# Layer B of a hybrid decoder step: decay rows by a transfer from DRAM, keys and values turned by VectorE's 32 x 32 transposes and on-chip transfers instead of by TensorE

## The chip, the cores and the metric

The kernel runs on one core of a Trainium2 chip. The metric is the device time of one execution in microseconds. Engines: TensorE (PE in the profile, its weight loads PEld), VectorE (DVE), ScalarE (ACT), GpSimd (POOL) and SyncE (SP), which here only issues DMAs.

## What is computed

One step of a two-layer decoder trunk for a prompt of 1024 tokens and a sample group of 8 x 4 tokens, all in float32. Layer A is windowed attention and is not touched. Layer B is gated DeltaNet: a short convolution on q, k and v, a decay per head, and the delta rule in chunks. The prompt part of it, per head and chunk of the kernel (128 tokens; the reference has 64, with the same result in exact arithmetic):

```
gc = cumsum(g)                                   # decay exponents of the chunk
decay[i, j] = exp(gc[i] - gc[j]) where j <= i
lmat = strict((k * beta) k^T * decay)
u, w = solve(I + lmat, [v * beta, k * beta * exp(gc)])
aqk  = (q k^T) * decay
v_new = u - w S
o     = (q * exp(gc)) S + aqk v_new
S     = S * exp(gc_last) + (k * exp(gc_last - gc))^T v_new
```

There are 8 heads of 128 columns and 8 chunks a head. Around it stand one projection (W_in), 4-head attention into 256 memory tokens, a gate and an output projection.

## The kernel before

The program is written in phases with a stream of instructions per engine and semaphores by hand. Layer B's phase (before.py from line 1888) works on "groups": group G is head G // 2, chunks 0 to 3 or 4 to 7, so there are NG_ = 16 of them. The main loop runs over G = 0 to 16 and in it over 16 slots. In pass G every engine does, slot by slot, the matrix part of group G (the products k k^T and q k^T, and the blockwise inverse of I + lmat, up to 128 x 128), the preparation of the next groups (convolution, norms, decays), and the state recurrence of group G - 1 (RSLOT: per chunk a step "a" with k S and q S, a step "b" with the inverse, a step "c" with the output and the state update). Between these TensorE issues "units": one product of 128 x 128 weights with 352 columns (in the profile two instructions, L2104) of the input projection of the head after. The table `slots` says how many units stand before and behind the recurrence's step in each slot: 36 in a pass up to G = 12, then 20, 16 and 20, since there is not much of the projection left; pass 16 has the rest and only the recurrence.

What the change touches:

- `to` (L2155) with r = None issues four TensorE transposes into one PSUM bank (L2160). Four results a group are made so. "ra": the cumulated decays `gc` of a chunk, one column broadcast to 128 x 128 and turned, so each partition has the row of all 128 exponents (slot 5, for G + 1). "kt" (slot 7) and "vt" (slot 15): keys and values of the four chunks, tokens to partitions. "ot" (slot 10): normed outputs; this one stays.
- VectorE reads them (`turned`, L2553): ra with the mask added into `ATs` (L2559), kt times a factor per token into `kdec` (L2567), vt times a factor into `vb` (L2570).
- ScalarE turns ATs to decays (`exps`, L2379, slot 7) behind the logs of norms (`norm_logs`, slot 5). kdec and vb are needed by the recurrence of the group, in the pass after.
- The inverse: VectorE's base steps on 16 x 16 blocks (`base_step`, L2629 and L2631) for group G + 1 in slots 12 to 15 of pass G and for group G in slots 0 to 5, then `base_turned` (L2636), which TensorE waits for in slot 7 (level x4, L2178). zz4, x5, zz5, x6, zt6 follow; `base_rows` (L2616, L2617) is a long transpose in slot 11 for the next group.
- PSUM banks 3 to 7 go round in the order of the list `work`; a step may be issued once the bank's fifth last user was read.
- SP loads weight blocks of 512 KB into a ring of four (`Ring.load`, L137), each once the block four before is used up, and stores a head's final state (`state_away`, L2076).
- GpSimd squares q and k, scales outputs, does the sample part of the convolution, and in passes 0 to 11 issues copies of window caches from DRAM to DRAM (`copy_part`).

Head by head the working data lie in fixed places: `qkvT` holds q, k and v of two heads with columns of the head on partitions and tokens along the row.

Of the kernel before, what the change touches and what calls it, by code (L numbers as in the profile page):

```python
# [27 lines left out]
HB = 8  # L28
# [86 lines left out]
class Chain:  # L115


    def __init__(self, nc, eng, name):
        self.eng, self.sem, self.n = eng, nc.alloc_semaphore(name), 0
# [27 lines left out]
def build(nc, ins, outs):  # L147
# [10 lines left out]
    part = dram("part", [2, SEQ, OW])  # L158
    memT_kept = dram("memT_kept", [P, KD * NMEM])
# [365 lines left out]
    def _(dve):  # L525
        own = Chain(nc, dve, "in_dve")
# [603 lines left out]
    def _(dve):  # L1130
        own = Chain(nc, dve, "dve_a")
# [168 lines left out]
    def _(pool):  # L1300
        own = Chain(nc, pool, "pool_a")
# [445 lines left out]
    def _(dve):  # L1747
        own = Chain(nc, dve, "wa_dve")
# [165 lines left out]
    S = take(2, P)  # L1914
    S_of = lambda h, c: S3[(NT * h + c) % 3]
# [14 lines left out]
    vb = mv[:, 0:2, :].rearrange("p a b -> p (a b)").rearrange("p (c e) -> p c e", e=P)  # L1930
    flat = lambda v: v.rearrange("p a b -> p (a b)")
# [49 lines left out]
    work = [(0, "ss"), (0, "ra"), (0, "kk"), (0, "qk")]  # L1981
# [12 lines left out]
    for n, (g, name) in enumerate(work):  # L1994
# [6 lines left out]
     cvs, spread, base, tap, chosen) = (  # L2001
# [4 lines left out]
            "diagonals_spread", "base_steps", "first_taps", "blocks_chosen"))  # L2006
# [43 lines left out]
    slots += [[(0, 1)] * 16, [(0, 2)] * 4 + [(0, 1)] * 12]  # L2050
# [24 lines left out]
    def _(sp):  # L2075
# [18 lines left out]
    def _(pe):  # L2094
# [102 lines left out]
        def chunk_step(g, s):  # L2197
# [9 lines left out]
            elif x == "b":  # L2207
                readout(pe, g, f"zt{LEVELS - 1}")
                readout(pe, g, f"ks{c}" if c else "vt")
                to(g, f"tr{c}", [(MT[:, c, :], r_sb[:, c % 2, :] if c else vb[:, c, :])])  # L2210
            elif x == "c":
                readout(pe, g, f"tr{c}")
                to(g, f"av{c}", [(ATs[g % 3][:, cl, :], vn[:, c % 2, :])])
                to(g, f"su{c}", [(kdec[:, c, :], vn[:, c % 2, :])])

        def turned(G, name):
# [11 lines left out]
            elif name == "kt":  # L2228
                to(G, "kt", [(ch(k_, c), None) for c in cs])
            elif name == "vt":  # L2230
                to(G, "vt", [(ch(v, c), None) for c in cs])
# [51 lines left out]
        turned(0, "ra")  # L2283
        for u in units[PER_HEAD + KD:PER_HEAD + 2 * KD]:
            unit(*u)
# [21 lines left out]
    def _(act):  # L2307
        def gate_piece(j):
# [3 lines left out]
            else:  # L2312
                act.wait_ge(ring.used, B2 + i + 1)
            if i == 2 and part_ == 0:
# [64 lines left out]
        def exps(G):  # L2379

            readout(act, G, "ra")
# [6 lines left out]
        def outputs(g):  # L2388

            b = left(act, g, "ot")  # L2390
            nc.scalar.activation(brT[:, g // 2, g % 2 * 512:(g % 2 + 1) * 512], b[:, :], ACT.Copy,
                                 scale=onw).then_inc(rd_act, 1)

# [64 lines left out]
        for G in range(NG_ + 1):  # L2458
            for s in SLOTS:
# [14 lines left out]
                if G == NG_ and s == 15:  # L2474
                    out_roots(NG_ - 1)
                for u in ended(units_at(G, s)):
# [12 lines left out]
    def _(dve):  # L2489
        own = Chain(nc, dve, "b_dve")  # L2490
# [62 lines left out]
        def turned(G, name):  # L2553
# [11 lines left out]
            elif name == "kt":  # L2565
                dve.wait_ge(hdv, 3 * G + 3)
                nc.vector.tensor_tensor(kdec[:, cs, :], bk(b), factors_of[:, KD_, cs].unsqueeze(2)  # L2567
                                        .to_broadcast([P, 4, P]), ALU.mult).then_inc(rd_dve, 1)
            elif name == "vt":
                nc.vector.tensor_tensor(vb[:, cs, :], bk(b), factors_of[:, KN, cs].unsqueeze(2)  # L2570
                                        .to_broadcast([P, 4, P]), ALU.mult).then_inc(rd_dve, 1)
# [66 lines left out]
        def chunk_step(g, s):  # L2638
# [4 lines left out]
            if x == "a" and c:  # L2643
                readout(dve, g, "vt")
# [86 lines left out]
        turned(0, "ra")  # L2731
# [1026 lines left out]
```

## Time and profile before

| | us |
|---|---|
| median of 3 runs | 2113.65 |
| lowest, highest | 2112.19, 2114.21 |
| the profiled execution, its own time | 2113.68 |
| its span in the profile | 2111.6 |
| TensorE busy | 2072.5 (98%) |
| VectorE busy | 997.2 (47%) |
| ScalarE busy | 697.7 (33%) |
| GpSimd busy | 454.6 (22%) |

The mean granted TensorE clock over the span is 0.993. Layer B's phase runs from about 1069 us to 1674 us; the first pass of its loop begins at about 1123 us, a pass takes about 34 us, and pass 13 begins at about 1555 us. In the profile "L2160" is a line of kernel.py; PSUM is "bank", all of SBUF is one tile "arena", so rows are told apart by their line.

### The profile page before, as it was taken

To read this page: it belongs to the slowest core of one execution; us is meant where nothing else is said; L and a number is where in the kernel's file an instruction comes from. 1 tells how busy PE (TensorE), PEld (TensorE's weight loads), DVE (VectorE), ACT (ScalarE), POOL (GpSimd) and SP (SyncE) were. 2 spreads that over 40 slices of the span, in tenths; PEclk is the share of its full clock that TensorE was granted. 3 is DMA by queue.
4 is the path that set the end of the run, shared out by engine and by line. 5 is a ranking of instruction groups with operands and counts; after the bars stand their busy time and mean duration, and the time that the engine had idled before them with its cause. 6 is when DMAs were issued, how large, how long until landed. Compare 5 with 4: busy or idle time off the path is not lost. (4 is left out here: it accounts for less than half of the span.)

```text
span 2111.6 us, 36594 instructions
## 1 busy us (share of the span) xinstructions
PE 2072.5 (98%) x14446; PEld 1487.2 (70%) x14446; DVE 997.2 (47%) x2664; ACT 697.7 (33%) x1631; POOL 454.6 (22%) x639
## 2 busy tenths in 40 slices
PE   8999999999999999999999999999999999999998
PEld 6888888888888887555466777767666666665444
DVE  5234354354435345331238777777876133332252
ACT  4121321322131122231135555555564344532101
POOL 0522232222223213300023134322331200020000
PEclk9999999999999999999999999999998999999999
DMA  7411301211131127668412122222210461134451
GB/s 235 161 43 41 107 27 51 80 41 43 41 97 37 50 83 223 237 202 255 131 31 74 73 95 83 93 87 82 73 48 13 137 256 31 41 105 134 134 161 50
DMA packets 210238, 210.34 MB, mean 100 GB/s; under 512 B 14261, under 2 KB 181653, under 8 KB 209150
## 3 DMA queue, kind: packets, MB, share of 16 engines
q1 hardware_dynamic: 198070, 148.27, 23.7%
q0 software_dynamic: 12000, 59.73, 7.4%
q8 instruction: 117, 1.92, 0.4%
q14 instruction: 51, 0.42, 0.1%
HBM read 179.56 MB, written 68.23 MB: 117 GB/s over the span
## 5 line engine op out<-in xcount | busy, mean ns | idle before, releaser
L887 PE MATMUL bank<-arena 128*128 128x256 f32 (+1 forms) x2688 | 631.7, 386 | 0.0
L887 PEld LDWEIGHTS bank<-arena 128*128 128x128 f32 x2688 | 494.5, 190 | 75.3
L2104 PE MATMUL bank<-arena 128*128 128x352 f32 x1296 | 452.5, 470 | 0.1
L2104 PEld LDWEIGHTS bank<-arena 128*128 128x128 f32 x1296 | 220.8, 191 | 71.4 <-issue 1.0
L2909 PE MATMUL bank<-arena 128*128 128x352 f32 x576 | 176.4, 459 | 0.0
L3399 PE MATMUL bank<-arena 128*128 128x512 f32 x360 | 167.5, 599 | 0.0
L2162 PEld LDWEIGHTS bank<-arena 128*128 128x128 f32 x864 | 129.9, 194 | 45.7 <-DVE arena L2646 3.7
L2909 PEld LDWEIGHTS bank<-arena 128*128 128x128 f32 x576 | 106.6, 190 | 53.3
L1341 POOL TENSOR_TENSOR arena<-arena 128x272 f32<-128x272 f32 (+1 forms) x48 | 31.5, 656 | 507.4 <-ACT arena L1061 487.4
L2162 PE MATMUL bank<-arena 128*128 128x128 f32 x864 | 135.0, 280 | 1.5 <-DVE arena L2646 1.0
L1323 POOL TENSOR_TENSOR arena<-arena 128x512 f32<-128x512 f32 x96 | 122.8, 1279 | 11.3 <-POOL arena L1323 0.9
L1660 PE MATMUL bank<-arena 128*128 128x512 f32 x248 | 118.6, 601 | 1.8 <-DMA arena<-in_w_out_a 1.8
L2508 DVE SCALAR_TENSOR_TENSOR arena<-arena 128x512 f32<-128x512 f32 x144 | 114.1, 793 | 0.7
L3399 PEld LDWEIGHTS bank<-arena 128*128 128x128 f32 x360 | 64.4, 189 | 70.4 <-issue 70.4
L924 PE MATMUL bank<-arena 128*128 128x128 f32 x396 | 79.3, 276 | 8.4 <-ACT arena L1096 7.2
L1096 ACT ACTIVATE arena<-arena 128x256 f32<-128x256 f32 (+1 forms) x128 | 59.9, 468 | 82.3 <-DVE arena L1185 74.5
L1169 DVE COPY arena<-bank 128x256 f32<-128x256 f32 (+1 forms) x208 | 78.8, 384 | 14.0 <-PE bank L924 14.0
L2631 DVE TENSOR_TENSOR arena<-arena 128x120 f32<-128x120 f32 (+14 forms) x240 | 76.2, 318 | 8.3
L924 PEld LDWEIGHTS bank<-arena 128*128 128x128 f32 x396 | 53.2, 141 | 29.8 <-ACT arena L1096 8.4
L1058 ACT COPY arena<-bank 128x272 f32<-128x272 f32 (+1 forms) x48 | 18.3, 381 | 166.7 <-PE bank L887 166.7
L1660 PEld LDWEIGHTS bank<-arena 128*128 128x128 f32 x248 | 42.2, 189 | 38.4 <-issue 34.7
L2808 POOL TENSOR_TENSOR arena<-arena 128x512 f32<-128x512 f32 x32 | 36.0, 1136 | 139.9 <-ACT arena L2352 139.9
(432 smaller groups left out, 2754.1 us busy)
## 6 DMA issues: line engine op xcount, KB each, us to landing
arena<-in_w_in_a SPq DMA_DIRECT2D x48, 512.0 KB, 5.2
arena<-in_w_in_b SPq DMA_DIRECT2D x40, 512.0 KB, 7.5
arena<-in_cache_win_k SPq DMA_DIRECT2D x48, 256.0 KB, 6.1
arena<-in_cache_win_v SPq DMA_DIRECT2D x48, 256.0 KB, 4.7
out<-arena SPq DMA_DIRECT2D x40, 256.0 KB, 3.4
arena<-in_w_mem_kv SPq DMA_DIRECT2D x16, 512.0 KB, 8.1
arena<-in_cache_mem_k SPq DMA_DIRECT2D x32, 256.0 KB, 4.3
arena<-in_cache_mem_v SPq DMA_DIRECT2D x32, 256.0 KB, 4.2
```

Of the source, the lines that this page charges most:

```text
L887: m = nc.tensor.matmul(o[:, 0:hi - lo], w, y, start=k == 0 and i in (0, 1, 3, 5), stop=k == KH - 1, skip_group_check=i in (2, 4, 6))
L924: m = nc.tensor.transpose(tB[e % 2][:, c * P:(c + 1) * P], src, ident)
L1096: nc.scalar.activation(pr[:, x % 2, c:256], sS[:, x % 2, c:256], ACT.Exp, bias=nm, accum_out=l).then_inc(p_done, 1)
L1169: nc.vector.tensor_copy(dst, tB[e % 2][:, lo:lo + w]).then_inc(t_read, 1)
L1323: nc.gpsimd.tensor_tensor(*v).then_inc(w_sums, 1)
L1660: i = nc.tensor.matmul(bank[BY0 + half][:, :], brT[:, k, n * P:(n + 1) * P], wo_a(k)[:, half * 512:(half + 1) * 512], start=j == 0, stop=j ...
L2104: m = nc.tensor.matmul(bank[j % 3][:, 0:PART], ring.slots[:, (B1 + b) % RING, k, :], part_in(k, part_), start=k == 0, stop=k == KD - 1)
L2162: m = nc.tensor.matmul(o[:, c * P:(c + 1) * P], l, r, start=True, stop=True)
L2508: x = nc.vector.scalar_tensor_tensor(out=dst, in0=src, scalar=cw, in1=dst, op0=ALU.mult, op1=ALU.add)
L2631: nc.vector.tensor_tensor(m[:, :, :, 0:j], m[:, :, :, 0:j], t, ALU.subtract).then_inc(base, 1)
L2909: m = nc.tensor.matmul(bank[part_][:, 0:PART], ring.slots[:, (B2 + b) % RING, k, :], part_in(k, part_), start=k == 0, stop=k == KD - 1)
L3399: m = nc.tensor.matmul(bank[BY0 + half][:, :], brT[:, k, n * P:(n + 1) * P], wo_b(k)[:, half * 512:(half + 1) * 512], start=j == 0, stop=j ...
```

## The change

Decay rows. Before group 0 TensorE turns `gc` once (64 columns: 8 chunks of 8 heads, "gr"), VectorE copies the 64 x 128 result, SP stores it in DRAM (`gc_kept`). For each group from 1 on SP loads four rows of it, broadcast to all 128 partitions, straight into ATs (`rows_to`: 128 x 4 pieces of 512 bytes, at the head of pass G for G + 1), and VectorE adds the mask to them in place (`mask_rows`) at the head of slot 6. ra remains for group 0 alone.

Keys and values. VectorE's stream transpose turns each 32 x 32 block in place of TensorE's 128 x 128 (`kv_turned`: one instruction of 128 x 512 for k in slot 6, one for v in slot 7, for group G + 1). The blocks must then change places across partitions: SP does it with 16 transfers a group, each of 32 partitions by 1 KB (`turned_to`). ScalarE scales the pieces into kdec and vb, two instructions a chunk, in slots 2 to 5 of the pass after (`scale_turned`). kt and vt are gone, with their slots and banks.

SP's program is written anew: the weight loads, the state stores and the new transfers in one order by pass. In pass 15 the four slots with two units are the last four and no longer the first four.

TensorE in pass 1, slots 5 to 8, before. L2160 is a quad of transposes (ra, then kt), L2162 x2 or x4 a product pair or kk, L2104 a unit, L2178 the inverse's x4:

```order
L2160 MATMUL bank<-arena 128x128 x4
L2104 MATMUL bank<-arena 128x352
L2162 MATMUL bank<-arena 128x128
L2104 MATMUL bank<-arena 128x352 x2
L2162 MATMUL bank<-arena 128x128 x2
L2104 MATMUL bank<-arena 128x352
L2160 MATMUL bank<-arena 128x128 x4
L2178 MATMUL bank<-arena 32x16 x16
L2104 MATMUL bank<-arena 128x352 x2
L2162 MATMUL bank<-arena 128x128 x4
```

And after, from the unit of slot 4 on (L2150 is the unit, L2208 a product, L2224 the inverse):

```order
L2150 MATMUL bank<-arena 128x352 x2
L2208 MATMUL bank<-arena 128x128
L2150 MATMUL bank<-arena 128x352 x2
L2208 MATMUL bank<-arena 128x128 x2
L2150 MATMUL bank<-arena 128x352
L2224 MATMUL bank<-arena 32x16 x16
L2150 MATMUL bank<-arena 128x352 x2
L2208 MATMUL bank<-arena 128x128 x4
```

Both quads are gone; the order of the rest is the same.

VectorE in a later pass, slot 5 to the head of slot 6, before: the read of ra (L2559) stands ahead of the last base steps, then the base's transpose and the two reads of the recurrence:

```order
L2508 SCALAR_TENSOR_TENSOR arena<-arena 128x512
L2559 TENSOR_TENSOR arena<-bank7,arena 128x512
L2629 TENSOR_TENSOR arena<-arena 128x8x2
L2631 TENSOR_TENSOR arena<-arena 128x8x2
L2629 TENSOR_TENSOR arena<-arena 128x8
L2631 TENSOR_TENSOR arena<-arena 128x8
L2636 STREAM_TRANSPOSE arena<-arena 128x128
L2652 TENSOR_TENSOR arena<-bank4,arena 128x128
```

After, the same place; the mask (L2660) comes behind the base's transpose (L2725):

```order
L2582 SCALAR_TENSOR_TENSOR arena<-arena 128x512
L2718 TENSOR_TENSOR arena<-arena 128x8x2
L2720 TENSOR_TENSOR arena<-arena 128x8x2
L2718 TENSOR_TENSOR arena<-arena 128x8
L2720 TENSOR_TENSOR arena<-arena 128x8
L2725 STREAM_TRANSPOSE arena<-arena 128x128
L2660 TENSOR_TENSOR arena<-arena 128x512
L2741 TENSOR_TENSOR arena<-bank3,arena 128x128
```

The base's transpose moved ahead of the 128 x 512 operation, the recurrence's reads did not.

VectorE right behind it, slots 6 and 7, before: the state update, four small factors, the read of kt (L2567) and of x4 (L2587), a convolution step:

```order
L2659 SCALAR_TENSOR_TENSOR arena<-arena,bank5 128x128
L2533 SCALAR_TENSOR_TENSOR arena<-arena 128x4
L2535 TENSOR_TENSOR arena<-arena 128x4
L2536 TENSOR_TENSOR arena<-arena 128x4
L2537 TENSOR_SCALAR arena<-arena 128x4
L2567 TENSOR_TENSOR arena<-bank6,arena 128x512
L2587 TENSOR_TENSOR arena<-bank7,arena 128x4x16
L2508 SCALAR_TENSOR_TENSOR arena<-arena 128x512
```

After:

```order
L2748 SCALAR_TENSOR_TENSOR arena<-arena,bank4 128x128
L2650 STREAM_TRANSPOSE arena<-arena 128x4x4x32
L2607 SCALAR_TENSOR_TENSOR arena<-arena 128x4
L2609 TENSOR_TENSOR arena<-arena 128x4
L2610 TENSOR_TENSOR arena<-arena 128x4
L2611 TENSOR_SCALAR arena<-arena 128x4
L2676 TENSOR_TENSOR arena<-bank5,arena 128x4x16
L2650 STREAM_TRANSPOSE arena<-arena 128x4x4x32
L2582 SCALAR_TENSOR_TENSOR arena<-arena 128x512
```

One transpose stands ahead of the factors, one behind the read of x4, and the read of kt is gone.

The core of the diff:

```diff
-    PREP = {5: ("ra",), 7: ("kt",), 8: ("kk",), 9: ("qk",), 15: ("vt",)}
-    NEXT = ("ra", "kk", "qk")
+    PREP = {8: ("kk",), 9: ("qk",)}
+    NEXT = ("kk", "qk")
+    AT_MASK = 6
+    AT_TURN = {6: 0, 7: 1}
+    SCALE_AT = {2: 0, 3: 1, 4: 2, 5: 3}
-    slots += [[(0, 1)] * 16, [(0, 2)] * 4 + [(0, 1)] * 12]
+    slots += [[(0, 1)] * 16, [(0, 1)] * 12 + [(0, 2)] * 4]
@@ SP
+        def rows_to(g):
+            h, c0 = g // 2, GR[g % 2][0]
+            if g > 2:
+                left(sp, g - 3, f"av{GR[(g - 3) % 2][1] - 1}")
+            sp.wait_ge(rows_away, 16)
+            if g > 1:
+                sp.wait_ge(rows_in, 16 * (g - 1))
+            src = gc_kept.rearrange("(c h) i -> h c i", h=HB)[h, c0:c0 + 4]
+            sp.dma_start(ATs[g % 3], src.unsqueeze(0).to_broadcast([P, 4, P])).then_inc(rows_in, 16)
+        def turned_to(g):
+            sp.wait_ge(turnd, 2 * (g + 1))
+            after(sp, kvs, 4 * g)
+            for b in range(4):
+                for a in range(4):
+                    sp.dma_start(kv_words[quarter(b), 256 * a:256 * a + 256],
+                                 turned_in[g][quarter(a), 256 * b:256 * b + 256]).then_inc(kv_in[g % 2], 16)
-        for b in range(3 * HB):
-            if b % 3 == 2 and b // 3 >= 3:
-                state_away(b // 3 - 3)
-            ring.load(sp, B1 + b + 1)
-        state_away(HB - 3)
-        ring.load(sp, B2 + RING)
+        for b in range(7):
+            weights(b)
+        readout(sp, 0, "gr")
+        sp.dma_start(gc_kept, gc_rows).then_inc(rows_away, 16)
+        turned_to(0)
+        for G in range(NG_):
+            if G + 1 < NG_:
+                rows_to(G + 1)
+            if G % 2 and G < NG_ - 1:
+                weights(3 * (G // 2) + 8)
+                weights(3 * (G // 2) + 9)
+            if G + 1 < NG_:
+                turned_to(G + 1)
+            if G % 2 == 0:
+                weights(3 * (G // 2) + 7)
@@ TensorE, tr0 and the state update
-                readout(pe, g, f"ks{c}" if c else "vt")
+                if c:
+                    readout(pe, g, f"ks{c}")
+                else:
+                    pe.wait_ge(kvs, 4 * g + 1)
+                pe.wait_ge(kvs, 4 * g + cl + 1)
                 to(g, f"su{c}", [(kdec[:, c, :], vn[:, c % 2, :])])
@@ ScalarE
+            if G:
+                act.wait_ge(masked, G)
+            else:
+                readout(act, 0, "ra")
+        def scale_turned(g, cl):
+            w, c = hd[:, g // 2 % 2], GR[g % 2][0] + cl
+            if not cl:
+                act.wait_ge(kv_in[g % 2], 256 * (g // 2 + 1))
+                act.wait_ge(hdv, 3 * g + 3)
+                if g > 1:
+                    left(act, g - 2, f"su{GR[g % 2][1] - 1}")
+            wide = lambda v: v.rearrange("p (a x) -> p a x", x=32)
+            nc.scalar.activation(wide(kdec[:, c, :]), kv_back[:, :, 0, cl, :], ACT.Copy, scale=w[:, KD_, c:c + 1])
+            nc.scalar.activation(wide(vb[:, c, :]), kv_back[:, :, 1, cl, :], ACT.Copy,
+                                 scale=w[:, KN, c:c + 1]).then_inc(kvs, 1)
@@ VectorE
+        def kv_turned(G, i):
+            h, gr = G // 2, G % 2
+            dve.wait_ge(sild, 3 * G + 2 + i)
+            if G and not i:
+                dve.wait_ge(kv_in[(G - 1) % 2], 256 * ((G + 1) // 2))
+            x = qkvT[:, h % 2, 1 + i, gr * 512:(gr + 1) * 512].rearrange("p (c b x) -> p c b x", c=4, b=4)
+            nc.vector.transpose(turned_kv[G][:, :, i].rearrange("p b c x -> p c b x"), x).then_inc(turnd, 1)
+        def mask_rows(G):
+            dve.wait_ge(rows_in, 16 * G)
+            nc.vector.tensor_tensor(ATs[G % 3], ATs[G % 3], wide4(mat(M_GE)), ALU.add).then_inc(masked, 1)
@@ VectorE, ahead of pass 0
         turned(0, "qk")
+        kv_turned(0, 0)
+        kv_turned(0, 1)
```

## Rows read from the trace of the kernel before

**Rows 1.** The page, part 1: busy us (share of the span) and instructions

```profile
PE 2072.5 (98%) x14446; PEld 1487.2 (70%) x14446; DVE 997.2 (47%) x2664; ACT 697.7 (33%) x1631; POOL 454.6 (22%) x639
```

**Rows 2.** Stretches: length, busy by engine (instructions), granted clock, DMA share, GB/s

```profile
1263.40:1297.70 34.30, 34.30 (x399) 24.19 (x398) 25.92 (x76) 19.31 (x46) 15.44 (x34) 1.00 0.29 95
...
1131.30:1543.30 412.00, 411.59 (x4842) 292.00 (x4842) 313.17 (x885) 226.23 (x540) 134.56 (x270) 1.00 0.23 83
1543.30:1640.00 96.70, 90.81 (x1163) 64.31 (x1162) 70.49 (x213) 46.94 (x117) 22.84 (x43) 0.93 0.12 30
```

**Rows 3.** L2160's instructions, then TensorE's timeline: start, length, instruction, [idle before]

```profile
L2160 PE MATMUL bank<-arena x256: 272/273/421, 1106.6 to 1673.5; 128*128 128x128 f32 x128
...
1226.02 0.60 PE L2160 MATMUL bank<-arena 128*128 128x128 f32 x4
1226.45 0.76 PE L2104 MATMUL bank<-arena 128*128 128x352 f32 x2
...
1229.49 0.60 PE L2160 MATMUL bank<-arena 128*128 128x128 f32 x4
1230.02 0.44 PE L2178 MATMUL bank<-arena 32*32 32x16 f32 x32
...
1232.66 0.73 PE L2178 MATMUL bank<-arena 32*32 32x16 f32 x64
...
1236.54 0.38 PE L2162 MATMUL bank<-arena 128*128 128x128 f32 x2
```

**Rows 4.** VectorE's timeline in the same pass, slots 5 to 7

```profile
1227.85 0.68 DVE L2559 TENSOR_TENSOR arena<-bank,arena 128x512 f32<-128x512 f32 x1
1228.45 0.16 DVE L2629 TENSOR_TENSOR arena<-arena 128x16 f32<-128x16 f32 x1
...
1229.29 0.31 DVE L2636 STREAM_TRANSPOSE arena<-arena 128x128 f32<-128x128 f32 x1
...
1230.99 0.21 DVE L2587 TENSOR_TENSOR arena<-bank,arena 128x64 f32<-128x64 f32 x1
```

**Rows 5.** VectorE's groups by shape, 1130 to 1620 us: busy, mean ns, idle before

```profile
L2617 DVE STREAM_TRANSPOSE arena<-arena 128x1920 f32<-128x1920 f32 x15 | 32.6, 2172 | 0.0
...
L2631 DVE TENSOR_TENSOR arena<-arena 128x112 f32<-128x112 f32 x15 | 13.8, 922 | 0.5
...
L2631 DVE TENSOR_TENSOR arena<-arena 128x120 f32<-128x120 f32 x15 | 4.3, 285 | 0.5
```

**Rows 6.** ScalarE's timeline: exps in slot 7, recurrence in slots 2 and 5

```profile
1232.24 1.28 ACT L2384 ACTIVATE arena<-arena 128x128 f32<-128x128 f32 x4
...
1256.08 0.40 ACT L2419 ACTIVATE arena<-arena 128x128 f32<-128x128 f32 x1 [2.77 <-DVE arena L2652]
...
1261.76 0.27 ACT L2414 COPY arena<-bank 128x128 f32<-128x128 f32 x1 [1.48 <-PE bank L2162]
```

**Rows 7.** VectorE's timeline, slot 8

```profile
1233.62 0.69 DVE L2562 TENSOR_TENSOR arena<-arena,bank 128x512 f32<-128x512 f32 x1 [1.76 <-ACT arena L2384]
...
1234.51 0.35 DVE L2646 SCALAR_TENSOR_TENSOR arena<-bank,arena 128x128 f32<-128x128 f32 x1
```

**Rows 8.** Timeline ahead of and in pass 0, VectorE and TensorE

```profile
1130.20 0.31 DVE L2636 STREAM_TRANSPOSE arena<-arena 128x128 f32<-128x128 f32 x1
...
1130.71 0.44 PE L2178 MATMUL bank<-arena 32*32 32x16 f32 x32
```

**Rows 9.** TensorE's timeline, passes 13 and 14

```profile
1581.40 0.64 PE L2170 MATMUL bank<-arena 64*32 64x64 f32 x16 [1.74 <-DVE arena L2604]
...
1584.28 1.22 PE L2162 MATMUL bank<-arena 128*128 128x128 f32 x4
...
1589.53 0.77 PE L2162 MATMUL bank<-arena 128*128 128x128 f32 x2 [0.69 <-DVE arena L2646]
```

**Rows 10.** SP's DMAs: the state's issue in ns, from issue to landing in us

```profile
L2078 SPq DMA_DIRECT2D out<-arena x8: 356/357/357, 1214.4 to 1663.1; - x8
...
DMA to landing us min/median/max: 1.5/8.5/11.6
```

More of the change, by code:

```diff
@@ L1914, in build @@
     S = take(2, P)
+    gc_rows = r_sb[0:64, 1, :]
     S_of = lambda h, c: S3[(NT * h + c) % 3]
@@ L1930, in build @@
     vb = mv[:, 0:2, :].rearrange("p a b -> p (a b)").rearrange("p (c e) -> p c e", e=P)
+    turned_in = [brT[:, HB - 2, 0:1024]] * (2 * HB - 1) + [xpad[:, 0, 0:1024]]
+    turned_kv = [w.rearrange("p (b i c x) -> p b i c x", b=4, i=2, c=4) for w in turned_in]
+    kv_words = sb[:, ZM[0]:ZM[0] + 1024]
+    kv_back = kv_words.rearrange("p (a i c x) -> p a i c x", a=4, i=2, c=4)
     flat = lambda v: v.rearrange("p a b -> p (a b)")
@@ L1980, in build @@
     reader_of = lambda n: "act" if n in ("ss", "ot") or n[:2] in ("qs", "tr") else "dve"
-    work = [(0, "ss"), (0, "ra"), (0, "kk"), (0, "qk")]
+    work = [(0, "ss"), (0, "ra"), (0, "gr"), (0, "kk"), (0, "qk")]
     for G in range(NG_ + 1):
@@ L2000, in build @@
     (pd, pr_, wk, rd_act, rd_dve, cvd, sild, sqd, hdv, hda, exd, mt0, onm, sqo, fac, tails, sqrt_o, cstep, xzero,
-     cvs, spread, base, tap, chosen) = (
+     cvs, spread, base, tap, chosen, rows_away, rows_in, masked, turnd, kv_even, kv_odd, kvs) = (
         sem(f"b_{n}") for n in (
@@ L2005, in build @@
             "out_factors", "conv_tails", "out_roots", "conv_steps", "buffers_zeroed", "samples_convolved",
-            "diagonals_spread", "base_steps", "first_taps", "blocks_chosen"))
+            "diagonals_spread", "base_steps", "first_taps", "blocks_chosen",
+            "rows_kept", "rows_loaded", "rows_masked", "kv_turned", "kv_moved_even", "kv_moved_odd", "kv_scaled"))
+    kv_in = (kv_even, kv_odd)
     s_out = stored["state"]
@@ L2213, in chunk_step, with decay_rows @@
                 to(g, f"av{c}", [(ATs[g % 3][:, cl, :], vn[:, c % 2, :])])
+                pe.wait_ge(kvs, 4 * g + cl + 1)
                 to(g, f"su{c}", [(kdec[:, c, :], vn[:, c % 2, :])])
+        def decay_rows():
+            o = bank_free(0, "gr")
+            nc.tensor.transpose(o[0:64, 0:P], gc[:, 0:64], ident).then_inc(wk, 1)
         def turned(G, name):
@@ L2283, in _ @@
         turned(0, "ra")
+        decay_rows()
         for u in units[PER_HEAD + KD:PER_HEAD + 2 * KD]:
@@ L2313, in gate_piece @@
                 act.wait_ge(ring.used, B2 + i + 1)
+            if i == 1 and part_ == 0:
+                act.wait_ge(kvs, 4 * NG_)
             if i == 2 and part_ == 0:
@@ L2475, in _ @@
                     out_roots(NG_ - 1)
+                if G < NG_ and s in SCALE_AT:
+                    scale_turned(G, SCALE_AT[s])
                 for u in ended(units_at(G, s)):
@@ L2564, in turned, with decay_rows @@
                 nc.vector.tensor_tensor(at_, at_, bk(b), ALU.mult).then_inc(rd_dve, 1)
[L2565 to L2571, printed above, removed]
+        def kv_turned(G, i):
[3 more added lines that the diff above has]
+                dve.wait_ge(kv_in[(G - 1) % 2], 256 * ((G + 1) // 2))
+            if G == NG_ - 1 and not i:
+                dve.wait_ge(cvd, 3 * NG_)
+                dve.wait_ge(tap, 3 * (NG_ - 2))
+            x = qkvT[:, h % 2, 1 + i, gr * 512:(gr + 1) * 512].rearrange("p (c b x) -> p c b x", c=4, b=4)
+            nc.vector.transpose(turned_kv[G][:, :, i].rearrange("p b c x -> p c b x"), x).then_inc(turnd, 1)
+        def decay_rows():
+            b = left(dve, 0, "gr")
+            nc.vector.tensor_copy(gc_rows, b[0:64, 0:P]).then_inc(rd_dve, 1)
+        def mask_rows(G):
+            dve.wait_ge(rows_in, 16 * G)
+            nc.vector.tensor_tensor(ATs[G % 3], ATs[G % 3], wide4(mat(M_GE)), ALU.add).then_inc(masked, 1)
         def matrix_step(G, s):
@@ L2731, in _ @@
         turned(0, "ra")
+        decay_rows()
         for w in range(CW):
@@ L2742, in _ @@
             for s in SLOTS:
+                if s == AT_MASK and G + 1 < NG_:
+                    mask_rows(G + 1)
                 if G < NG_:
@@ L2746, in _ @@
                     chunk_step(G - 1, s)
+                if s in AT_TURN and G + 1 < NG_:
+                    kv_turned(G + 1, AT_TURN[s])
                 if s == AT_INV:
```

33 lines of the change are left out of this document (16 added, 17 removed).

## The prediction

> **What bounds the kernel now.** I read first the busy time by engine [rows 1]: TensorE's matmul record covers 98% of the span, no other engine passes 47%. That alone says little, so I looked at the stage that the change touches in stretches [rows 2]. From 1131.3 to 1543.3 us TensorE is busy 411.6 of 412.0 us at full granted clock; a group of four chunks (one pass of the loop over G) takes 34.3 us, VectorE works 25.9 us of it and ScalarE 19.3. The stretch from 1543.3 to 1640 is different: TensorE is busy 90.8 of 96.7 us and the mean granted clock is 0.93. So I count twelve "dense" groups (G = 1 to 12), where what TensorE does not issue is time gained, and treat G = 0 and the tail (G = 13 to 15) by themselves. I write slot s for the sixteen steps of a group.
>
> **What is removed from TensorE.** 16 times kt, 16 times vt, 15 times ra: 47 quads of transposes. L2160 has 256 records of one pass each [rows 3], that is 64 quads (the rest are ot and ra(0)). Price of one quad: the quad at 1226.02 is followed by the next product at 1226.45, so 0.43 us [rows 3]. The quad at 1229.49 is followed by the inverse's tiled products at 1230.02, 0.53 us [rows 3]; I put the 0.10 more down to the step to tiled products, which stays, and take 0.43 there too. A dense group loses 3 quads, 1.29 us, of 34.3. The mean of 275 ns of one record is its length in the pipeline, not its price. If all 47 quads counted: 20.2 us. Added: one transpose before G = 0, 0.15 us.
>
> **Does anything come late in a dense group?** I walk the group around 1230 us. Slot 7's x4 needs base_turned (L2636), which ends at 1229.60 while TensorE starts x4 at 1230.02 [rows 4, 3]. Two quads less bring TensorE there at about 1229.15. But VectorE no longer reads ra (L2559) in slot 5: 1227.85 to the next start at 1228.45 is 0.60 us [rows 4], and L2636 ends at 1229.00. The mask now stands behind it: 0.1 to 0.15 us are left.
> VectorE then has, in slots 6 and 7: the mask (128x512, both sources in SBUF). The nearest row is the read of ra, 128x512 with one source in a bank, 0.68 us [rows 4]; 128x120 in SBUF takes 0.28 [rows 5], the same pace. I take 0.68. Two stream transposes of 128x512: the rows have 128x128 at 0.31 [rows 4] and 128x1920 at 2.17 us [rows 5], 1.04 ns an element, so 0.71; the upper end is four times the small one, 1.24. Removed are the reads of kt and vt, of the form of ra's, 0.68 each. VectorE's sum per group: plus 0.68 plus 1.42 minus 2.04, nothing. In order: the output read L2652 starts where it did, the first transpose costs 0.65, the kt read gives back 0.60, and the x4 read (L2587, ending at 1231.20 [rows 4]) ends at about 1231.25. TensorE wants it for zz4 at 1232.66 minus 0.86 = 1231.80 [rows 3]: 0.55 left.
> ScalarE gets eight scalings of 128x128 in slots 2 to 5. Nearest: the exps, 128x128 in SBUF with an operand per partition, four in 1.28 us, and 0.27 to 0.40 us for single ones [rows 6]. I take 0.32, so 0.65 a slot and 2.6 a group: 21.9 us of 33. Slots 2 and 5 have idle of 2.77 and 1.48 us there [rows 6]. In slot 5 the pair stands ahead of the logs, and so of exps: later by 0.65, earlier by the 0.43 of ra, net 0.2. VectorE waited 1.76 us for those exps at 1233.62 [rows 7]. The use of L2646 (ended at 1234.86) at TensorE's step at 1236.54 had 1.7 us of slack [rows 7, 3]; minus 0.86 minus 0.2 leaves 0.6. So I keep the full 1.29 us in each dense group: **12 x 1.29 = 15.5 us.** If the small slacks are wrong by half a microsecond, this is where it costs.
>
> **G = 0.** VectorE works without a gap up to the end of L2636 at 1130.51 [rows 8]. kv_turned(0) puts 1.4 us into that stretch, the ra read takes 0.6 out: L2636 ends at 1131.3. TensorE started x4 at 1130.71 [rows 8] and would be ready at 1129.85. It starts at 1131.35: the two quads bring nothing and 0.6 us is lost; vt gives 0.43 back. **Minus 0.2 us**, and 0.15 for the added transpose.
>
> **Tail.** In G = 13 and 14 few projections are left, and TensorE waits for VectorE, longest 1.74 us at x6 [rows 9]. Two microseconds later the same steps take twice as long (four passes of a state step 1.22 us [rows 9]), the 1.2 GHz level, for about 13 us. In G = 13 VectorE waits for exps, which do not get earlier, and then runs without a gap into the next group: no gain up to x6. vt's read goes, and the wait of 0.69 at 1589.53 [rows 9] ends 0.6 earlier. G = 14 can use two quads and vt's, less what exps hold back: about 0.9 more. In G = 15 two quads bring 0.86, but four products (2.35 us, 0.59 each) move from slots 0 to 3 to slots 12 to 15, while VectorE's base steps fill slots 0 to 4: TensorE arrives earlier than it can be served and loses an estimated 1.1. Sum of the tail: 0.6 + 0.9 + 0.9 - 1.1 = **1.3 us**; ends: 0 and 4.7 (all eleven quads outside the dense groups).
>
> **Transfers.** Per group SP issues 16 small ones (32 partitions of 1 KB) and one of 256 KB. An issue takes 0.36 us [rows 10], 16 take 5.8. The only small transfer in this stage lands after 1.5 to 11.6 us, median 8.5, beside the cache copies [rows 10]: the last kv piece is there 6 to 18 us after the second transpose, at about 1231.9. ScalarE asks for it in slot 2 of the next group, behind L2419 at 1256.08 [rows 6], 24 us later. Cost taken: 0, hidden by those 24 us. Behind it on SP stand the next rows (needed in slot 6 of the following group) and the weight blocks; a block waits for slot 14 of an even group or slots 1 and 4 of an odd one, which is before or after these issues, and has some 30 products until its use. Behind ScalarE's wait stand the copy of tr1 (L2414, slot 5) and the reads of projections, on which TensorE waits; some 2.5 us of that are free.
>
> **Sum.** 15.5 - 0.2 - 0.15 + 1.3 = 16.4 us. The profiled execution took 2113.68 us (span 2111.6), its median of runs 2113.65, so no correction: **2097.3 us.**
>
> **Rivals.**
> A, small slacks are used up. VectorE's operation with both sources in SBUF takes 0.92 instead of 0.28 us where GpSimd works beside it (L2631, [rows 5]). The mask is such an operation: 0.65 more at the head of slot 6 turns 0.55 of slack at zz4 into a wait, the longer transposes (1.24) do the same. 0.1 to 1.1 us in each dense group; at 0.6, 7 us: 2104.5. Against: GpSimd's long operations are not in slot 6.
> B, a second stretch at the low clock. The tail has less TensorE work than before between waits. G = 14, with one projection a slot, kept the full clock; whether narrowly the rows cannot tell. The 13 us stretch at 1.2 GHz cost at most 6.6; another of such length, partly behind VectorE, 4: 2101.
> C, slower: kv lands late. It decides from 26.5 us after the transpose (24 and the 2.5 free). Each us above costs 15 us over the run, 27.6 us is the break-even, 29 us gives 37.5 - 16.4 = 21.1 more: 2135. For it: the landing times are from a transfer in a queue shared with copies, and sixteen in a row, each 1.5 us if they ran one after the other, would be 24 us, just in time. Against: issues of 0.36 us and overlapping landings.
> The Trainium skill, "DMA: Bandwidth & Descriptors", section "Rules for kernel authors", says that transfers below 64 KB pay mostly overhead, and its section "Anatomy of one DMA" has a fixed part of about 2.0 us. Paid one after another, 16 x 2.0 = 32 us, an estimate from that page, would be late; no row here shows sixteen in a row.
> D, no effect: the matmul record is not the bound and the freed time becomes waiting. It gives 2113.7. For it: weight loads are busy only 24.2 of 34.3 us [rows 2]. Against: TensorE has next to no idle, and its quads have a pitch.
> The Trainium skill, "Perfetto Trace Analysis", section "Identifying the Most-Contended Engine", calls matmul busy time a poor measure of the distance to peak and prefers weight load time; by that, 71% here, TensorE would have room. It speaks of the distance to peak, not of whether the next step waits.
> E, the tail gains more: the low-clock stretch shrinks, or all quads count: 20.2 us, 2093.5.
>
> **How the numbers follow.** Forecast 0.58, A 0.14, B 0.10, C 0.07, D 0.05, E 0.06. A measurement of this kernel tells about 0.2%, 4 us, from no change. Faster: forecast, A, B, E: 0.88; the same: D, 0.05; slower: C, 0.07. The range goes from E with a little of the clock back, 2092.5, to A, 2105.5, and leaves out C, D and some of A.
>
> **What would show it.** In the profile after, the interval between two groups of the dense stretch is 33.0 us, not 34.3 (A: 33.5 or more, with a TensorE wait at x4 or zz4; C: a ScalarE wait for a transfer at the scaling in slot 2). L2160's place has 69 records instead of 256. G = 0 shows a wait of over 1 us for the base transpose. VectorE's new transposes show 0.71 us (or up to 1.24), ScalarE's scalings 0.32 to 0.40, the sixteen transfers a last landing below 24 us after the second transpose. The forecast is wrong if the dense interval stays at 34 us, or if the tail has more than 14 us at the low clock.

## The result and the profile after

The changed kernel takes 2333.3 us (median of 4 runs, 2330.7 to 2334.0) against 2112.9 for the kernel before (2111.9 to 2114.2): ratio 1.104, 95% interval 1.102 to 1.106. Its profiled span is 2331.8 us. It is slower by 10%, 220 us, where 16 us less were forecast.

The page of the kernel after, lines of its parts 1 (against [rows 1]), 2 and 5:

```profile
PE 2067.1 (89%) x14259; PEld 1474.5 (63%) x14259; DVE 1002.1 (43%) x2665; ACT 731.9 (31%) x1759; POOL 451.9 (19%) x639
...
PE   8999999999999999999394764949478999999998
...
PEclk9999999999999999999797977979798999999999
...
L2208 PE MATMUL bank<-arena 128*128 128x128 f32 x864 | 140.7, 287 | 190.8 <-ACT arena L2418 185.8
...
L2462 ACT ACTIVATE arena<-arena 128x128 f32<-128x128 f32 x64 | 25.4, 397 | 235.4 <-DMA arena<-arena 235.4
```

TensorE works no longer than before and stands still in layer B's slices, every other one. The last row shows what it comes from: ScalarE, at the first scaling of a group (L2462), waited 235.4 us for a transfer within SBUF. Its waits between 1100 and 1860 us, us in total, times, longest:

```profile
ACT arena L2462 <- DMA arena<-arena: 235.4, 7, 40.3
...
PE bank L2208 <- ACT arena L2418: 185.8, 6, 34.9
```

Seven waits in sixteen groups: pass 0 and then every second pass. Stretches of the kernel after (columns as in [rows 2]), one between two waits and one in a wait:

```profile
1186.00:1219.00 33.00, 33.00 (x388) 23.11 (x388) 25.55 (x72) 20.12 (x52) 11.42 (x25) 1.00 0.25 85
1219.00:1262.00 43.00, 8.91 (x33) 5.90 (x33) 6.17 (x22) 6.78 (x18) 1.03 (x1) 0.60 0.19 68
```

Between the waits a group runs as forecast, without a gap. In the wait TensorE is busy 8.9 of 43 us, at a mean granted clock of 0.60. SyncE's timeline there (start, length, transfers), then the waits that end it, on ScalarE and TensorE:

```profile
1189.71 0.37 SPq L139 DMA_DIRECT2D arena<-in_w_in_b  x1
1195.99 37.94 SPq L2107 DMA_DIRECT2D arena<-arena  x16
1234.03 0.52 SPq L2099 DMA_DIRECT2D arena<-gc_kept  x1
1264.43 11.36 SPq L2107 DMA_DIRECT2D arena<-arena  x16
```

```profile
1255.65 0.40 ACT L2462 ACTIVATE arena<-arena 128x128 f32<-128x128 f32 x1 [35.63 <-DMA arena<-arena]
```

```profile
1258.59 0.77 PE L2208 MATMUL bank<-arena 128*128 128x128 f32 x2 [34.09 <-ACT arena L2418]
```

The 16 transfers of one group take 11.4 us to issue, those of the group before it 37.9, and ScalarE gets the last piece 59.7 us after the first was issued. The difference between the two is GpSimd's cache copies: it issued one at 1189.1 and one at 1211.5 us; the packets of the first ran until 1230, those of the second until 1253.3 us, each copy about 40 us; at 1264 none was in flight. (The landing that the profile gives for the first, 24.0 us, is too early: all copies count on one semaphore, and 1213.1 is 1.6 us after the second was issued.) What goes through the DMA engines meanwhile, 1200 to 1210 us (q0 is GpSimd's queue, q1 SyncE's; packets, MB, share of 16 engines):

```profile
DMA packets 17, 0.54 MB, mean 54 GB/s; under 512 B 0, under 2 KB 8, under 8 KB 8
## 3 DMA queue, kind: packets, MB, share of 16 engines
q0 software_dynamic: 8, 0.52, 12.0%
...
q1 hardware_dynamic: 8, 0.00, 0.1%
```

In 10 us eight packets of 64 KB (0.52 MB) and eight small ones of SyncE's. The copy keeps 12.0% of 16 engines busy, two engines, with a packet of 64 KB in 2.4 us, and SyncE gets one small packet through for each. From 1213 to 1230 us both copies ran, on four engines; just behind the end of the second only SyncE's packets are left, 93 in 2.5 us, and ScalarE goes on at 1255.65 (1213 to 1230 us, then 1253.5 to 1256 us):

```profile
DMA packets 195, 1.82 MB, mean 107 GB/s; under 512 B 50, under 2 KB 168, under 8 KB 168
...
q0 software_dynamic: 26, 1.69, 23.1%
```

```profile
DMA packets 93, 0.05 MB, mean 20 GB/s; under 512 B 12, under 2 KB 93, under 8 KB 93
...
q1 hardware_dynamic: 93, 0.05, 8.1%
```

Six of ScalarE's seven waits end 1.9 to 2.9 us behind the last packet of the copies in flight: at one small packet for each 2.4 us, what SyncE has on a copy's two engines gets through only when the copy is over. In the Trainium skill, "DMA: Bandwidth & Descriptors", section "Queues, rings and completion order" has each DMA engine take turns between queues by whole packets, and "Why a DMA increments its semaphore by 16 and not by 1" has a transfer use as many engines, up to 16, as divide its slowest dimension, which is 2 for a copy of two batches. The trace agrees with both; only, the page gives a packet typically 9 to 17 descriptors, and what passes here at a turn is one record of the profile, 512 bytes or 1 KB.

### The profile page after: what moved, and what is told of

It is laid out like the page before. It is cut to its first block, busy times and chain, and to the rows that moved or that the text cites. A ratio compares the mean times of both kernels' runs of the same rounds, so it can differ in the third digit from the quotient of the medians.

```text
span 2331.8 us, 36733 instructions
## 1 busy us (share of the span) xinstructions
PE 2067.1 (89%) x14259; PEld 1474.5 (63%) x14259; DVE 1002.1 (43%) x2665; ACT 731.9 (31%) x1759; POOL 451.9 (19%) x639
## 4 chain that ended last, share of the span: by engine, by line
PE 33%; SPq 10%; DMA 6%; DVE 3%; ACT 1%; issue 1%; DVEq 0%; ACTq 0%
PE bank L2150 10%; SPq L2107 10%; PE bank L3005 7%; PE bank L3495 7%; DMA arena<-arena 6%; PE bank L2208 2%; PE bank L2224 1%; PE bank L3021 1%; PE bank L3030 1%; PE bank L3473 1%; DVE arena L2720 1%; PE bank L2216 1%; PE bank L3506 0%; DVE arena L2582 0%; DVE arena L2650 0%
## 5 line engine op out<-in xcount | busy, mean ns | idle before, releaser
L888 PEld LDWEIGHTS bank<-arena 128*128 128x128 f32 x2688 | 494.5, 190 | 75.3
L2150 PE MATMUL bank<-arena 128*128 128x352 f32 x1296 | 458.9, 479 | 0.1
L2208 PE MATMUL bank<-arena 128*128 128x128 f32 x864 | 140.7, 287 | 190.8 <-ACT arena L2418 185.8
L2208 PEld LDWEIGHTS bank<-arena 128*128 128x128 f32 x864 | 133.8, 200 | 240.7 <-issue 193.1
L2150 PEld LDWEIGHTS bank<-arena 128*128 128x128 f32 x1296 | 227.9, 195 | 79.4 <-issue 4.5
L3005 PE MATMUL bank<-arena 128*128 128x352 f32 x576 | 176.4, 459 | 0.0
L3005 PEld LDWEIGHTS bank<-arena 128*128 128x128 f32 x576 | 106.6, 190 | 53.3
L1324 POOL TENSOR_TENSOR arena<-arena 128x512 f32<-128x512 f32 x96 | 122.7, 1278 | 11.1 <-POOL arena L1324 0.9
L3495 PEld LDWEIGHTS bank<-arena 128*128 128x128 f32 x360 | 64.4, 189 | 70.4 <-issue 70.4
L2462 ACT ACTIVATE arena<-arena 128x128 f32<-128x128 f32 x64 | 25.4, 397 | 235.4 <-DMA arena<-arena 235.4
L925 PE MATMUL bank<-arena 128*128 128x128 f32 x396 | 79.3, 276 | 8.4 <-ACT arena L1097 7.2
L1097 ACT ACTIVATE arena<-arena 128x256 f32<-128x256 f32 (+1 forms) x128 | 59.7, 467 | 82.4 <-DVE arena L1186 74.5
L2910 POOL TENSOR_TENSOR arena<-arena 128x512 f32<-128x512 f32 x16 | 16.5, 1033 | 338.8 <-DVE arena L2625 338.8
L925 PEld LDWEIGHTS bank<-arena 128*128 128x128 f32 x396 | 53.2, 141 | 29.8 <-ACT arena L1097 8.4
```

The costliest lines, as they stand in the source:

```text
L888: m = nc.tensor.matmul(o[:, 0:hi - lo], w, y, start=k == 0 and i in (0, 1, 3, 5), stop=k == KH - 1, skip_group_check=i in (2, 4, 6))
L925: m = nc.tensor.transpose(tB[e % 2][:, c * P:(c + 1) * P], src, ident)
L1324: nc.gpsimd.tensor_tensor(*v).then_inc(w_sums, 1)
L2150: m = nc.tensor.matmul(bank[j % 3][:, 0:PART], ring.slots[:, (B1 + b) % RING, k, :], part_in(k, part_), start=k == 0, stop=k == KD - 1)
L2208: m = nc.tensor.matmul(o[:, c * P:(c + 1) * P], l, r, start=True, stop=True)
L3005: m = nc.tensor.matmul(bank[part_][:, 0:PART], ring.slots[:, (B2 + b) % RING, k, :], part_in(k, part_), start=k == 0, stop=k == KD - 1)
```

## The experiments

Theory 1, formed on this profile: each of the 16 transfers passes one long packet, so the lateness is their number times 2.4 us. Theory 2: the copy's bytes leave no room. Theory 3: SyncE's order of waits is the cause, the copies are not. Theory 4 was formed later and is stated where it arose. Each quoted text is what was expected before its run.

**The copies over all engines.**

```
-        copy_cache(pool, src, dst, 512, drop, (n % 4 * 2,))
+        for b in (n % 4 * 2, n % 4 * 2 + 1):
+            pool.dma_start(dst[0, b, ..].rearrange("(s x) -> s x", s=16), src[0, b, ..] ...)
```

> The kernel after, with each of the twelve early cache copies issued as two transfers of 16 rows, so that their bytes go over all DMA engines in place of two; the 16 small transfers of each group are as they were. Theory 1 (the small transfers each pass behind a long piece on the two engines that carry a copy): the pieces of a group come back to about 11 us of issue, ScalarE's waits for them (235.4 us in all) are nearly gone, the dense part is 33.0 us a group, and the time is near 2100 us (2092 to 2125). Theory 2 (the copy's bytes, whatever their engines, leave the small transfers no room): 2300 us or more. Theory 3 (SyncE's order of waits is the cause, the copies are not): 2333 us, unchanged.

> The kernel before with the same cache copies over all DMA engines: the base for the run above. Theories 1 to 3 all expect no change from before, 2112 to 2116 us, since no small transfer of layer B is waited for there; if spread copies cost or bring something by themselves, it shows here.

Measured: 2105.3 us for the changed kernel (ratio to before 0.9964, 0.9953 to 0.9974), 2113.5 for the kernel before (0.9997, 0.9987 to 1.0008). One edit of GpSimd's copies takes 228 us from the changed kernel and nothing from the other. In the changed kernel with spread copies the small transfers take 0.59 us each, and the median landing of all 256 is 1.9 us; 1184 to 1194 us, beside a copy:

```profile
L2109 SPq DMA_DIRECT2D arena<-arena x256: 507/591/2909, 1115.4 to 1603.0; - x128
...
  ACT arena L2464: 9.6, 1
...
DMA to landing us min/median/max: 1.8/1.9/7.2
```

```profile
DMA packets 588, 2.36 MB, mean 236 GB/s; under 512 B 43, under 2 KB 555, under 8 KB 555
...
q0 software_dynamic: 59, 2.08, 48.5%
```

Theories 2 and 3 fall: the bytes and the order are the same, the rate is more than four times as high (236 against 54 GB/s), and what is left is one wait of 9.6 us in pass 0.

**No copies in layer B.** `NUM_EARLY = 12` becomes `0`.

> The kernel after with none of the cache copies in layer B's stage: all are issued in the later part of the program. Theories 1 and 2 (a copy in flight makes the small transfers late): ScalarE's 40 us waits are gone, the two-pass period is back at 66 to 68 us from 101.7, the time near 2100 us, if the later part takes the copies in at no cost; the cost is bounded by the next run of this kind on the kernel before. Theory 3 (SyncE's order): about 2333 us.

Measured: 2156.4 us (1.0207, 1.0191 to 1.0223). Layer B is free of waits for kv but the first (7.1 us). The loss came back in the later phase, where the copies now stand beside its weight loads:

```profile
PE bank L3005 <- DMA arena<-in_w_in_b: 51.0, 2, 46.5
```

So a copy as it is written also delays a weight load, here by up to 46.5 us. The expectation had near 2100 only if the later part took the copies at no cost, and it did not; I did not run the kernel before in this form.

**One transfer a group, and half of the transfers.**

```
-            for b in range(4):
-                for a in range(4):
-                    sp.dma_start(kv_words[quarter(b), ..], turned_in[g][quarter(a), ..])
+            sp.dma_start(kv_words, turned_in[g])      # first;  in the second: for a in range(2)
```

> The kernel after with one transfer of 128 rows x 4 KB a group in place of the 16 small ones: the same bytes, but the sixteenths don't change places, so keys and values are the wrong ones. The copies stay as they are. Theory 1 (the cost is the number of transfers times a long piece): one transfer passes one or two pieces, lands some 5 to 10 us late, which the 24 us of cover take, and the time is 2095 to 2115 us. Theory 2 (bytes): 2333 us, unchanged. Theory 3 (SyncE's order of waits): 2333 us, unchanged.

> The kernel after with its copies on two DMA engines as they were, but only 8 of the 16 transfers of each group (half of the keys' and values' pieces are not moved, so the products of layer B are wrong ones). If the lateness is so many transfers times one long piece, the row of issues falls from 37 to about 19 us, the last piece lands some 20 us after the transposes, inside the 24 to 26 us of cover, and the time is near 2105 us. If it is one long piece for each row that a transfer puts on those two engines, whatever the number of transfers, it falls to half too, but one transfer of all the bytes took 38.5 us; so between the two only the size counts: a time above 2200 would say that the number of transfers does not set it.

Measured: 2218.6 us (1.0502, 1.0481 to 1.0523) and 2301.8 (one execution). One transfer in place of 16 still landed late, here the one issued at 1192.4 us:

```profile
L2105 SPq DMA_DIRECT2D arena<-arena x1: 472/472/472, 1192.4 to 1192.4; - x1
...
DMA to landing us min/median/max: 38.5/38.5/38.5
```

and half of them took 32.8 us to issue in place of 37.9. So Theory 1's count is wrong. That transfer landed at 1230.9 us, and the packets of the copy issued at 1185.5 ended at 1228.0: this run alone can't tell whether a copy holds its engines to its end, but the eight small packets between eight long ones above say that it doesn't. **Theory 4:** what counts is SyncE's small packets on the two engines, one for each packet of 64 KB, all that stand ahead in the queue included: weight blocks and decay rows are packets too. The weight block issued at 1189.7 in the kernel after landed 42.7 us later, at 1232.4, behind the end of the first copy. By this, their number counts only as long as an engine has fewer of them than the copy has long ones left; beyond that the copy's end decides.

**Shorter packets, same bytes.** Copies described in pieces of 8 KB side by side; then each copy as two transfers, with every other piece of 4 KB:

```
+        parts = [v.rearrange("b (s i x) -> b s i x", i=2, s=(512 - drop) // 4) for v in (dst.., src..)]
+        for i in range(2):
+            pool.dma_start(parts[0][:, :, i], parts[1][:, :, i])
```

> The kernel after with its twelve early copies each still one transfer of two batches, but described in pieces of 8 KB in place of 64 KB; kv and everything else as in the kernel after. Theory 4 (on an engine that carries a copy, one packet of SyncE's queue passes for each piece of the copy, and a piece of 64 KB takes 2.4 us; all of SyncE's packets ahead count, the weight blocks' too): a piece of 8 KB takes about an eighth, 0.3 us, so the last piece of kv is there in time and the time is 2100 to 2110 us, even if the copy stays on two engines. A theory in which any copy in flight on the same engine holds the queue until it is over: above 2250 us, unless the shorter pieces also go over all engines; the rate (134 GB/s on two engines) would show which.

> The pieces of 8 KB of the run with short pieces lay next to one another and went as packets of 64 KB after all, so it repeated the kernel after. Here each copy is two transfers, one with every other 4 KB piece, the other with the rest, so that no packet can be longer than 4 KB; kv, weights and order are those of the kernel after. Theory 4 (one packet of SyncE's queue passes for each packet of the copy): a packet of 4 KB takes about 0.2 to 0.3 us in place of 2.4, so no lateness is left even on two engines, and the time is 2100 to 2115 us. Theory 2 (bytes leave no room) and a theory by which a copy holds its engines until it is over: 2300 us or more.

Measured: 2333.7 us (1.1045, 1.1028 to 1.1062) and 2136.6 (1.0104, 1.0087 to 1.0121). The first edit did nothing: 1199 to 1209 us shows the same 8 packets with 0.52 MB, so pieces side by side had gone as 64 KB. The second did:

```profile
DMA packets 1117, 1.29 MB, mean 129 GB/s; under 512 B 476, under 2 KB 916, under 8 KB 1115
## 3 DMA queue, kind: packets, MB, share of 16 engines
q0 software_dynamic: 459, 0.82, 21.2%
q1 hardware_dynamic: 656, 0.45, 17.0%
```

Beside more bytes of copy than the kernel after had in such a stretch (0.82 MB, 1204 to 1214 us), 656 packets of SyncE's pass in place of 8 (on all 16 engines; 216 of them, and 260 of the copy's 459, are under 512 bytes), the transfers issue in 10 to 12 us, and ScalarE waits once (11.5 us, pass 0). That is Theory 4's mechanism, by packet length. The two halves of a copy ran at once, up to four of their packets at a time, so more engines carried a copy than before, not fewer. The time is over the 2100 to 2115 expected, because GpSimd twice could not issue a transfer (25.3 us, and 28.0 at 1497.1), and TensorE stood behind it, 15.9 and 8.4 us; those two passes took 51.8 and 43.5 us where 33 is usual. The first:

```profile
1255.36 1.08 POOL L321 DMA_DIRECT2D out<-in_cache_win_k  x1 [25.31 <-issue]
```

```profile
1257.57 1.11 PE L2210 MATMUL bank<-arena 128*128 128x128 f32 x4 [15.86 <-POOL arena L2914]
```

What held these issues is open; q0's packets had gone from 12000 to 73440.

**Decay rows alone, copies spread.** Keys and values back on TensorE.

> Only the decay rows come by the transfer; keys and values are turned on TensorE as before, in before's slots; cache copies are spread over all DMA engines as in the earlier run. It tells how much of the gain is the fifteen quads of the rows and whether the rows alone bring a loss. By the prediction's price of 0.43 us a quad: 12 x 0.43 = 5.2 us in the dense groups, at most 1.3 at the ends, so 2106 to 2109 us. If the quads of the rows bring nothing (the mask on VectorE takes it back), 2113.

Measured: 2106.3 us (0.9965, 0.9953 to 0.9977), as expected. Its twelve dense groups take 403.1 us against 408.4 of the kernel before: 0.44 less a group, the price of one quad.

**Pass 0.** Spread copies, and kv through DRAM (one store, four loads), or turned earlier on VectorE:

```
-        kv_turned(0, 0)                 # stood behind turned(0, "qk")
-        kv_turned(0, 1)
         norm_inverses(0)
+        kv_turned(0, 0)
...
         decay_rows()
+        kv_turned(0, 1)
```

> Spread copies, and a group's keys and values go by one store to DRAM and four loads back in place of 16 transfers within SBUF: 5 issues in place of 16, two landings one after the other. If the 9.6 us that ScalarE still waited in pass 0 came from 16 issues of 0.6 to 0.8 us behind one another (12.6 us), the wait falls to about 2 to 3 us and the time to 2098 to 2101 us. If it came from the landing alone, two landings make it longer: 2106 or more.

> Spread copies, 16 transfers as before, but VectorE turns the keys and values of pass 0 earlier: the keys ahead of the convolution of the next head's queries, the values behind the copy of the decay rows. The first piece can then leave at about 1109.6 instead of 1115.4 us, ScalarE's wait of 9.6 us in pass 0 falls to about 4, and TensorE gets back 3 to 4 of the 5.5 us that pass 0 lost: 2101 to 2103 us. If pass 0 was not late for that wait, no change against 2105.3.

> The version with spread copies and pass 0's keys and values turned early (2099.1 us), with the copies in pieces of 8 KB in place of 64 KB. Theory 4: what is left of ScalarE's wait in pass 0 (6.1 us, 16 issues in 14.3 us beside a copy, 10.8 us without) falls by up to 3.5 us, and 1 to 2 of them come back at TensorE: 2097 to 2099 us. If short pieces slow the copies or the weight blocks: above 2101.

> As the run before, and kv by one store to DRAM and four loads back. The store leaves at about 1108 us, its landing takes 2.5 to 3 us, the four loads 4 to 5: ScalarE has the pieces by its request at 1116 to 1118 us, the wait in pass 0 is gone, and the time is 2096 to 2099 us. The dense part should stay at 32.8 us a group, since 24 us of cover hide either form.

Measured: 2102.8 us through DRAM (0.9949, 0.9934 to 0.9963), ScalarE's wait 7.5 us where 2 to 3, and 2098 to 2101 us, were expected: the loads left at 1115.2 us, beside the halves of a copy issued at 1111.7; 2099.1 turned early (0.993, 0.9919 to 0.9942), wait 6.1, where 4 and 2101 to 2103 us were expected. The pieces of 8 KB again went as 64 KB, so the third is the second once more: 2100.0 (0.9938). The fourth has both, and its copy leaves at 1114.9 us behind the loads: no wait for kv is left in pass 0, and 2099.2 (0.9936, 0.9924 to 0.9949), the upper end of what was expected.

Its profiled execution saved less than its wait because one group beside a spread copy took 36.1 us, where its neighbours take 32.5 to 33.0. The two stretches, and TensorE's row at its start:

```profile
1313.58:1346.36 32.78, 32.59 (x385) 22.69 (x385) 26.23 (x75) 21.11 (x52) 9.16 (x17) 1.00 0.28 93
1346.36:1382.47 36.11, 34.82 (x390) 24.31 (x389) 26.25 (x74) 21.16 (x54) 13.54 (x31) 0.95 0.47 151
```

```profile
1360.39 0.31 PE L2228 MATMUL bank<-arena 32*32 32x16 f32 x16 [1.29 <-issue]
```

A stop of 1.3 us for nothing that the profile shows, and behind it a lower granted clock, 0.95 in the mean of the group. The version turned early without DRAM has the same stop, 1.3 us, at a clock of 1.00, and its group took 34.5; the other version through DRAM took 36.4 (stop 1.6, clock 0.95), the first spread version 34.2 (stop 1.0). Without copies the group took 33.0, without a stop. So the stop goes with the spread copy, and the low clock was seen only in the two versions through DRAM; what makes either was not tested.

## Why the prediction was wrong

**The step that failed is the one under "Transfers": "Cost taken: 0, hidden by those 24 us."** It took the landing times from the one small store near by, at most 11.6 us [rows 10], and the issue at 0.36 us, and so had the last piece there 6 to 18 us after the second transpose. Beside the copies it was there 59.7 us after the first piece was issued (1195.99 to 1255.65), and ScalarE waited 35.6 us for it; for the group issued at 1264.43, with no copy in flight, nobody waited. The row that answered the question was in the same trace, for a load of SyncE's that starts beside a copy. Kernel before, the weight block at 1292.7 us, 0.7 us behind a copy issued at 1292.05:

```profile
L139 SPq DMA_DIRECT2D arena<-in_w_in_b x1: 368/368/368, 1292.7 to 1292.7; - x1
...
DMA to landing us min/median/max: 43.5/43.5/43.5
```

It landed at 1336.2 us. Nobody waited for it, since some 30 products stood before its use, so it was in no view of waits. The change put transfers that are waited for after 24 us into the same queue. I looked at how small the transfer was, not at what else was on its engines. The two sections of the Trainium skill named above bear on that; the prediction weighed only the fixed cost of about 2.0 us, which the section that it cites gives for transfers issued by GpSimd. With the copies spread, the median of SyncE's 256 landings was 1.9 us: the fixed cost was not the trouble.

**Rival C** had the right mechanism on the surface (a ScalarE wait in slot 2, kv past 26.5 us) and a chance of 0.07; it put the lateness down to sixteen fixed costs. Its price was wrong on both sides: landing at 29 us where it was 60, and fifteen late groups where there were seven. During a stop of about 34 us the copies come to their end, so the next group is in time and the two-pass period is 101.7 us. Seven long passes against before's 34.0 (30.1 in pass 0) make +36, five times +34 to +36, and +17 us: 228, less some 8 that the other passes saved, is the 220 measured.

**Dense groups: right.** Between the same steps of TensorE (L2193, L2241) the twelve groups from pass 0's end took 408.4 us before and 394.5 with spread copies, 13.8 less; 393.5 without copies, 14.9 less. Forecast: 15.5. The forecast of 33.0 a group was met (32.5 and 33.0 in turn), but the 34.3 that it stood against was one group; before's mean is 34.03. The prices by part, kernel after: transpose 0.70 us (forecast 0.71), mask 0.65 (0.68), scalings at 1255.65 and 1255.96 a pitch of 0.31 (0.32):

```profile
L2650 DVE STREAM_TRANSPOSE arena<-arena x32: 669/701/706, 1111.2 to 1820.4; 128x512 f32<-128x512 f32 x32
```

```profile
L2660 DVE TENSOR_TENSOR arena<-arena x15: 648/651/665, 1161.9 to 1818.2; 128x512 f32<-128x512 f32 x15
```

Of rival A's small slacks only the one at x4 was used up, in two of the twelve groups and by 0.5 us in all; TensorE's waits from 1157.4 to 1551.9 us with spread copies:

```profile
PE bank L2226 <- issue: 1.0, 1, 1.0
PE bank L2226 <- DVE arena L2727: 0.5, 2, 0.3
```

**G = 0: wrong size.** Forecast -0.2 us; pass 0 took 35.7 us with spread copies against 30.1, -5.7, and 32.6 without copies, -2.5. The 24 us of cover hold from G = 1 on. In pass 0 the transposes end at 1115.4 us and ScalarE asks at 1119.8: 4.4 us, for 16 issues of 0.6 us or more. I had walked G = 0 for VectorE and TensorE, not for the transfers. Turned early and through DRAM, pass 0 took 28.9 us, 1.2 less than before, better than the forecast.

**Tail: 1.3 us less was forecast, and it got longer.** The pass behind the dense groups, with spread copies and, for comparison, what the trace of before has for it:

```profile
1551.95:1583.01 31.06, 25.08 (x349) 17.54 (x348) 26.32 (x73) 19.60 (x51) 11.10 (x25) 0.89 0.23 60
```

```profile
1560.31:1591.40 31.09, 26.72 (x361) 19.23 (x361) 25.95 (x74) 17.53 (x43) 11.28 (x25) 0.87 0.14 38
```

TensorE has 1.6 us less to do and the pass is as long as it was: here, where it waits for VectorE (3.7 us at L2218), rival D holds, which the dense groups refute. From the start of that pass to the end of layer B, the kernel before and the version turned early with the copies in pieces of 8 KB, which have the same mean granted clock:

```profile
1560.31:1673.47 113.16, 107.27 (x1143) 76.28 (x1143) 59.31 (x190) 51.76 (x128) 24.71 (x44) 0.94 0.13 36
```

```profile
1546.74:1661.52 114.78, 104.74 (x1111) 72.40 (x1111) 58.65 (x188) 58.44 (x152) 24.51 (x45) 0.94 0.17 46
```

That is 1.6 us more. Which step of the tail's walk failed was not tested. With decay rows alone it was 110.2 us at a mean clock of 0.97, with spread copies 113.5 at the same clock, so the loss comes with the keys and values, or with the four slots of two units that were put last with them. The stretch at the low clock differs from trace to trace: 13.7 us before, 6.8 with spread copies, 17.1 turned early, 3.4 of them a second stretch at 1606.8 us. That is rival B in small, and over the 14 us that the prediction named as a sign of being wrong. Rival E did not come up.

**Sum** with spread copies: 0.2 (ahead of pass 0) - 5.7 + 13.8 + 0 (pass 13) - 0.3 (behind it) = 8.0 us; span 2103.5 in place of 2111.6. Once the transfers have their cover, 2099.1 was reached, 14.4 us below the kernel before of the same round, where 16.4 had been forecast. In its trace 3.1 us of that lie ahead of pass 0, where the change does next to nothing, 0.5 in pass 0 and 13.6 in the dense groups, and 3.2 are lost behind them. The dense groups are the change's worth; that the total came near the forecast is in part luck.

## What to carry to other kernels

Before a transfer is put on a path that someone waits for, look up the longest landing of any transfer of the same queue, unwaited ones above all (43.5 us here), and what else was in flight then. A large DRAM to DRAM copy should be described so that it uses all DMA engines: here the slowest dimension 16 in place of 2 changed nothing in one kernel and 228 us in the other. Cover has to be counted for the first pass by itself.

## What the runs showed of the hardware

- A DMA engine that carries a copy in packets of 64 KB (2.4 us each) let one small packet of another queue pass for each: 8 and 8 in 10 us. With packets of 4 KB, and all 16 engines counted, 459 and 656.
- Six of seven waits for small transfers ended 1.9 to 2.9 us behind the last packet of such a copy.
- Pieces of 8 KB side by side went as packets of 64 KB; pieces of 4 KB kept apart did not.
- The same copy took about 40 us on two engines, and its halves landed after 5.9 to 12.0 us on all.
- Where several transfers count on one semaphore, the landing that the profile gives can be too early: 24.0 us for a copy whose packets ran for about 40.
- Issues of 16 transfers within SBUF take 0.59 us each, where a store to DRAM took 0.36 [rows 10].
